# A two-block transformer forward pass on one core: the HGRN scan's steps set half a turn apart, the small gates moved into its first projection, and the low parts of weights issued one panel later

## The chip, the cores and the metric

The kernel runs on one core of one Trainium2 chip. The metric is the device time of one execution in microseconds (us). Before the change three runs took 2718.82, 2721.54 and 2724.38 us, so the median is 2721.54 us.

TensorE (PE) multiplies, VectorE (DVE), ScalarE (ACT) and GpSimd (POOL) work elementwise, and SyncE (SP) issues the weight transfers.

## The reference

Two models run one after the other on 256 tokens of 1024 features, each with two layers, all in float32. The first is attention with three branches; the second has an SSD branch, an HGRN branch and an mLSTM branch, and then a feed-forward part. The change touches the HGRN branch and the small gates of the other two:

```python
q = silu(q_raw);  v = i_in                       # 8 heads of 128
f = lb + (1.0 - lb) * sigmoid(f_raw)             # forward and backward
k = (1.0 - lb) * sigmoid(-f_raw)
o_f = scan(q, k[0], v, log f[0])                 # o_t = sum_s<=t (q_t . prod f . k_s) v_s
o_b = flip(scan(flip(q), flip(k[1]), ...))
o = group_rmsnorm(o_f + o_b) * silu(g_out)
dt = softplus(dt_raw + dt_bias);  A = -exp(a_log)     # small gates: SSD
ig = i + i_bias;  log_f = log_sigmoid(f + f_bias)     # small gates: mLSTM
```

## The kernel before, in words

**Weights.** Every projection is cut into 768 panels of 1024 weights for each partition (512 KB). SP loads panel i into a ring of five slots (`wring`). ACT rounds it to the high part `whi`, DVE subtracts to get the low part `wlo`; both have four slots. PE makes three products for each tile (high by high, high by low, low by high). A panel is two tiles of columns with four chunks of rows, or the like: 24 matmuls.

**Order.** `schedule` writes one list of steps. Each engine's program walks this list and issues, in that order, its own part of every step. Nothing is reordered later: an instruction that waits holds up all that its engine has behind it. `weave((a, 1), (b, 1.2))` interleaves generators: at each turn `a` advances one `yield`, `b` 1.2 on average. A projection (`projB`) yields after each panel and again after its output step.

**Split.** At the step `panel i` the list gets `split` of panel i + 3 (`LEAD`). ACT's half waits until the transfer has landed and until PE is done with panel i - 1, whose slot it takes (`NS` = 4). DVE's half waits for ACT's half. SP's transfer of panel p waits for the low part of panel p - 5.

**HGRN scan.** Four heads at a time (`hg_scan`, twice for each layer), the 256 tokens' decays are built in levels j = 0 to 6. One level has four parts:
- `hg_scale j` (DVE): four multiplies of half of `hgQF`, `hgkf`, `hgQB`, `hgkb` by the products of decays `hgTf` and `hgTb`, and two shorter ones that make the next `hgTf`, `hgTb`.
- `hg_merge j+1`: ACT makes three copies of halves into `hgQm` and `hgKm`, POOL one. It waits for `hg_scale j` and for the products of level j - 1, whose buffers it takes; `hg_scale j+1` waits for it.
- `hg_products j`: eight float32 matmuls of 128x128 (16 instructions) on PE, once `hg_merge j` is done.
- the same step on DVE: two predicated copies from PSUM into `hgA`.

Ahead stand the first product (j = -1) and `hg_split`; behind stand `hg_cross`, `hg_values` and `hg_norm`.

**Order around the scan.** For each layer: the first half's projections (`hg_proj(0)`, 20 panels) alone; then its scan woven with the small gates and the second half's projections (20 panels); then the second scan woven with two gates' projections (16 panels). The small gates are one narrow panel, some 15 short DVE operations, four ACT operations with three different function tables, short matmuls for running sums, and a running maximum in eight steps of four short DVE operations.

`forget_out` stands for two parts: ACT's two sigmoids, and DVE's six operations that scale them.

Of the kernel before, what the change touches and what calls it, by code (L numbers as in the profile page):

```python
# [315 lines left out]
def run(g):  # L316
    for _ in g:
        pass
# [89 lines left out]
def schedule(K, a):  # L408
# [439 lines left out]
    def block2(l, norm):  # L848
# [4 lines left out]
        rms_turn(norm, l, "norm_mix_g_2", uT)  # L853

        def small_gates():
            tb = ar.take("smallT", 256, at=7168)
# [4 lines left out]
            yield  # L861
            do("ssd_skip", c, AB.take())
            yield
            yield
            yield
            do("cumsum_rows", c, AB.take(), AB.take())
# [12 lines left out]
            do("ml_max_cols", c, AB.take())  # L879
            do("store_max", c)  # L880
            yield
# [3 lines left out]
        def hg_proj(hf, B):  # L885
            c0, o = hf * 512, 17920 * hf
            B.q = ar.take("hgq", 1024, at=o)
            yield from projB(w, GQ + c0, 512, uT, features_to(B.q, ACT.Silu))
            fk, kk = B.f, B.kf = ar.take("hgf", 1024, at=o + 1024), ar.take("hgkf", 1024, at=o + 3072)
            yield from projB(w, GF + c0, 512, uT, lambda k, m, u: do("forget_out", c, fk, kk, hf * 4, k, u))  # L890
            fk, kk = B.b, B.kb = ar.take("hgb", 1024, at=o + 2048), ar.take("hgkb", 1024, at=o + 4096)
            yield from projB(w, GF + 1024 + c0, 512, uT, lambda k, m, u: do("forget_out", c, fk, kk, 8 + hf * 4, k, u))
            B.v = ar.take("hgv", 1024, at=o + 5120)
            yield from projA(w, GI + c0, 512, uT, tokens_to(B.v, 512))
            B.g = ar.take("hgg", 1024, at=o + 6144)
            yield from projB(w, GG + c0, 512, uT, features_to(B.g, ACT.Silu))

        def hg_scan(hf, B, W):
# [3 lines left out]
            do("hg_start", B)  # L902
            do("hg_products", B, -1, [AB.take(), AB.take()])
            do("hg_split", B)
            do("hg_merge", B, 0)
            yield
            for j in range(7):
                do("hg_scale", B, j)
                if j < 6:
                    do("hg_merge", B, j + 1)  # L910
                yield
                do("hg_products", B, j, [AB.take(), AB.take()])
                yield
            do("hg_cross", B, [AB.take(), AB.take()])
            ar.give(B.q, B.f, B.b, B.kf, B.kb)
            if hf:
                ar.give(*W.Tf, *W.Tb, *W.QK[1])
            yield
            for h in range(0, 4, 2):
# [145 lines left out]
        B0, B1 = Box(), Box()  # L1065
        run(hg_proj(0, B0))
        yh = ar.take("yh", 2048, at=25104)
        c.sm, c.mxb = ar.take("sm", 688, at=31360), ar.take("mxb", 1024, at=32048)
        c.rows = ar.take("rows", 512, at=33072)

        c.spread = {}
        RS = Slots([c.mxb.part("spread", 0, 512), c.mxb.part("spread", 512, 512), c.rows.again("spread")])

        def spread_rows(i):
            if i < 24:
                c.spread[i] = RS.take()
                do("spread_rows", c, i, c.spread[i])
        s, mxb = c.sm.ap, c.mxb.ap
        c.par = K.parb[:, 128 * l:128 * l + 112]
        c.ds = K.parb[0:1, 128 * l + 112:128 * l + 128].rearrange("p (c j) -> p j c", j=2)  # L1080
        v2 = lambda o, n: s[:, o:o + n].rearrange("p (t k) -> p t k", t=2)
        c.raw, c.z, c.za, c.dts, c.LA, c.ncum, c.R, c.em = (
            v2(0, 128), v2(128, 96), v2(224, 96), v2(320, 96), v2(416, 96), v2(512, 96), v2(608, 32), v2(640, 32))
        c.Dc, c.nA = s[:, 672:680], s[:, 640:672]
        c.ldt = c.z[:, :, 0:32]

        c.mA = mxb[0:8, 0:512].rearrange("p (d t) -> p d t", d=2)
        c.mB = mxb[0:8, 512:1024].rearrange("p (d t) -> p d t", d=2)
        c.nmx = c.mA
        W = hg_work()  # L1090
        weave((hg_scan(0, B0, W), 1), (small_gates(), 0.8), (hg_proj(1, B1), 1.2))

# [425 lines left out]
def scalar_program(e, K, sg, a):  # L1518
# [3 lines left out]

    def split(p):
        w, hi, lo = p.flat
# [205 lines left out]

    def forget_out(c, fk, kk, i0, k, u):
        e.wait_ge(*at(u.full))
# [129 lines left out]
    parts = dict(split=split, load_first=load_first, load_second=load_second, columns=columns, rope_tables=rope_tables,  # L1862
                 lower_bounds=lower_bounds, split_bank=split_bank, split_bank_scaled=split_bank_scaled, features_out=features_out,
# [13 lines left out]
def vector_program(e, K, sg):  # L1877
# [3 lines left out]

    def split(p):
        w, hi, lo = p.flat
# [308 lines left out]
    def small_gates(c):  # L2192
# [11 lines left out]
        e.wait_ge(*now(chain))  # L2204
        e.tensor_tensor(c.za, c.za, c.z, ALU.min).then_inc(*up(chain, ("za", c.l)))
        e.wait_ge(*at(("softplus", c.l)))
        e.tensor_scalar(c.z, c.z, 0.0, None, ALU.max).then_inc(*up(chain))
# [49 lines left out]

    def forget_out(c, fk, kk, i0, k, u):
        e.wait_ge(*at("bounds"))
# [20 lines left out]

    def hg_products(B, j, us):
        for st in range(2):
# [227 lines left out]

    parts = dict(split=split, rope_tables=rope_tables, lower_bounds=lower_bounds, split_bank=split_bank, split_bank_scaled=split_bank_scaled,
                 latent_out=latent_out, latent_norm=latent_norm, kpe_out=kpe_out, mla_rope=mla_rope, scores=scores, weights=weights,
# [3 lines left out]
                 ssd_skip=ssd_skip, cumsum_cols=cumsum_cols, ml_key_gates=ml_key_gates, ml_max_rows=ml_max_rows,  # L2516
                 ml_max_step=ml_max_step, ml_max_negate=ml_max_negate, ml_max_cols=ml_max_cols, forget_out=forget_out, hg_start=hg_start,
                 hg_products=hg_products, hg_split=hg_split, hg_scale=hg_scale, hg_norm=hg_norm, ssd_conv=ssd_conv, ssd_products=ssd_products, ssd_exponents=ssd_exponents, ml_exponents=ml_exponents, ssd_weights=ssd_weights,
                 ssd_outputs=ssd_outputs, ssd_norm=ssd_norm, ml_weights=ml_weights, ml_outputs=ml_outputs, ml_variance=ml_variance, ml_norm=ml_norm,
# [193 lines left out]
```

## Time and profile before

| | |
|---|---|
| median of three runs | 2721.54 us |
| profiled execution, its own time | 2726.25 us |
| its span on the core | 2724.4 us |
| PE busy | 2526.3 us (93%) |
| DVE busy | 1808.3 us (66%) |
| ACT busy | 1433.4 us (53%) |
| POOL busy | 226.7 us (8%) |
| mean granted TensorE clock | 0.967 |
| read from HBM | 422.35 MB |

The span is the time from the first to the last instruction that the profiler saw. PE is busy nearly all the time, so the time goes where PE is idle, or where its clock is granted at half. In the second model layer 0 begins near 1098 us and layer 1 near 1906 us; the HGRN stretch is 1110 to 1372 us in the one and ends at 2182 us in the other.

### The profile page before, as it was taken

To read this page: it belongs to the slowest core of one execution; us is meant where nothing else is said; L and a number is where in the kernel's file an instruction comes from. 1 tells how busy PE (TensorE), PEld (TensorE's weight loads), DVE (VectorE), ACT (ScalarE), POOL (GpSimd) and SP (SyncE) were. 2 spreads that over 40 slices of the span, in tenths; PEclk is the share of its full clock that TensorE was granted. 3 is DMA by queue.
4 is the path that set the end of the run, shared out by engine and by line. 5 is a ranking of instruction groups with operands and counts; after the bars stand their busy time and mean duration, and the time that the engine had idled before them with its cause. 6 is when DMAs were issued, how large, how long until landed. Compare 5 with 4: busy or idle time off the path is not lost.

```text
span 2724.4 us, 42235 instructions
## 1 busy us (share of the span) xinstructions
PE 2526.3 (93%) x17296; PEld 2312.2 (85%) x17296; DVE 1808.3 (66%) x2928; ACT 1433.4 (53%) x2099; POOL 226.7 (8%) x193
## 2 busy tenths in 40 slices
PE   7998999999989999879899979999979899979998
PEld 7887889988779898778899778998878898778997
DVE  4556676555566755657677777875567677776875
ACT  4555545545464544446455534664545556535654
POOL 0000000000000000000024510000000025410000
PEclk9999999999999999889899989999989999989999
DMA  7553456655435566533367635665624467635663
GB/s 226 155 140 102 138 172 191 192 155 162 119 92 166 171 205 202 143 93 109 109 190 185 170 105 172 187 202 172 171 74 114 115 198 196 168 99 173 192 199 131
DMA packets 358958, 426.24 MB, mean 156 GB/s; under 512 B 21208, under 2 KB 286894, under 8 KB 358766
## 3 DMA queue, kind: packets, MB, share of 16 engines
q1 hardware_dynamic: 342890, 401.95, 49.2%
q10 hardware_dynamic: 14068, 15.91, 2.7%
q0 software_dynamic: 1808, 5.69, 0.7%
q8 instruction: 137, 2.24, 0.3%
q14 instruction: 55, 0.45, 0.1%
HBM read 422.35 MB, written 1.15 MB: 155 GB/s over the span
## 4 chain that ended last, share of the span: by engine, by line
PE 68%; DVE 18%; ACT 9%; issue 4%; DMA 1%; ACTq 0%; POOL 0%; DVEq 0%
PE ps L112 66%; DVE wlo L121 4%; ACT whi L118 3%; DVE sE L121 2%; PE ps L115 2%; ACT hgKm L118 1%; DVE hgA L148 1%; ACT E L118 1%; DVE hgQF L121 1%; ACT L118 1%; DVE hgQB L121 1%; DVE E L124 1%; DVE hgkf L121 1%; DVE xN L121 1%; DVE hgkb L121 1%
## 5 line engine op out<-in xcount | busy, mean ns | idle before, releaser
L121 DVE TENSOR_TENSOR wlo<-wring,whi 128x1024 fp32r<-128x1024 f32 x768 | 925.6, 1217 | 581.9 <-ACT whi L118 581.5
L118 ACT ACTIVATE whi<-wring 128x1024 fp32r<-128x1024 f32 x768 | 800.8, 1053 | 419.8 <-PE ps L112 410.7
L112 PE MATMUL ps<-uT,whi 128*128 128x256 f32 x4640 | 835.4, 284 | 12.7 <-DVE uT L121 9.1
L112 PEld LDWEIGHTS ps<-uT,whi 128*128 128x128 f32 x4640 | 723.4, 193 | 20.3 <-issue 19.2
L112 PE MATMUL ps<-uT,wlo 128*128 128x256 f32 x2320 | 654.1, 282 | 0.0
L112 PEld LDWEIGHTS ps<-uT,wlo 128*128 128x128 f32 x2320 | 446.2, 192 | 0.0
L112 PE MATMUL ps<-xT,whi 128*128 128x256 f32 x2112 | 387.6, 287 | 4.7 <-DVE xT L121 4.0
L112 PEld LDWEIGHTS ps<-xT,whi 128*128 128x128 f32 x2112 | 328.6, 191 | 12.2 <-issue 7.8
L112 PE MATMUL ps<-xT,wlo 128*128 128x256 f32 x1056 | 299.4, 284 | 0.0
L112 PE MATMUL ps<-whi,hid 128*128 128x512 f32 x864 | 267.8, 389 | 0.0
L112 PEld LDWEIGHTS ps<-xT,wlo 128*128 128x128 f32 x1056 | 202.9, 192 | 0.5
L112 PEld LDWEIGHTS ps<-whi,hid 128*128 128x128 f32 x864 | 162.2, 188 | 33.3
L112 PE MATMUL ps<-wlo,hid 128*128 128x512 f32 x432 | 168.1, 389 | 0.0
L112 PE MATMUL ps<-whi,xT 128*128 128x512 f32 x384 | 132.2, 406 | 0.0
L124 POOL TENSOR_SCALAR sE<-mxb,sm 128x256 f32<-128x256 f32 x64 | 109.6, 1721 | 270.8 <-DMA mxb<-spread 258.8
L112 PE MATMUL ps<-whi,uT 128*128 128x512 f32 x384 | 127.9, 404 | 0.0
L118 ACT ACTIVATE E<-ps,E 128x256 f32<-128x256 f32 x112 | 52.1, 472 | 119.1 <-DVE E L124 118.9
L112 PE MATMUL ps<-hgQm,hgKm 128*128 128x128 f32 x448 | 67.2, 311 | 40.1 <-ACT hgKm L118 33.0
L118 ACT ACT_TABLE_LOAD x77 | 98.8, 1283 | 3.3 <-issue 1.8
L112 PEld LDWEIGHTS ps<-hgQm,hgKm 128*128 128x128 f32 x448 | 62.6, 222 | 43.2 <-ACT hgKm L118 35.0
L112 PEld LDWEIGHTS ps<-wlo,hid 128*128 128x128 f32 x432 | 81.1, 188 | 16.5
L118 ACT ACTIVATE hgQm<-hgQF 128x512 f32<-128x512 f32 x28 | 17.9, 640 | 138.9 <-DVE hgTb L121 114.9
(377 smaller groups left out, 3670.4 us busy)
## 6 DMA issues: line engine op xcount, KB each, us to landing
wring<-in_w_in SPq DMA_DIRECT2D x346, 512.0 KB, 4.0
wring<-in_mlp_w SPq DMA_DIRECT2D x128, 512.0 KB, 4.4
wring<-in_w_up SPq DMA_DIRECT2D x88, 512.0 KB, 4.4
wring<-in_w_down SPq DMA_DIRECT2D x44, 512.0 KB, 3.9
wring<-in_w_branch SPq DMA_DIRECT2D x32, 512.0 KB, 3.6
wring<-in_w_out SPq DMA_DIRECT2D x32, 512.0 KB, 3.9
wring<-in_mem_w_kv SPq DMA_DIRECT2D x16, 512.0 KB, 5.2
wring<-in_w_br_hg SPq DMA_DIRECT2D x16, 512.0 KB, 4.4
```

What stands on the lines that cost most here:

```text
L112: return self.e.matmul(*p, **k) if self.e else Nothing()
L115: return self.e.transpose(*p, **k) if self.e else Nothing()
L118: return self.e.activation(*p, **k) if self.e else Nothing()
L121: return self.e.tensor_tensor(*p, **k) if self.e else Nothing()
L124: return self.e.tensor_scalar(*p, **k) if self.e else Nothing()
L148: return self.e.copy_predicated(*p, **k) if self.e else Nothing()
```

## The change

Four things change in the list of steps; no arithmetic is added or removed.

1. Steps of the scan. `hg_products` becomes two steps: the matmuls keep the name and come directly behind `hg_scale j` in the list; the copies into `hgA` become `hg_level j`. Between the two there is a yield, and `hg_merge j+1` moves from directly behind `hg_scale j` to behind that yield. So the list reads: scale j, products j, (other work), merge j+1, level j, (other work), scale j+1.
2. `forget_out` is cut in two: DVE's part is `forget_scale`, issued at the next output instead of its own.
3. The small gates are woven into `hg_proj(0)`, seven yields late, and no longer into the first scan. Their DVE part is split in two (`small_gates`, `small_rates`).
4. `split` becomes `split_hi` (panel i + 3, as before) and `split_lo` (panel i + 2). This holds for all 768 panels of both models.

```diff
+        if pend: do("forget_scale", *pend.pop())      # in forget's out()
 ...
             do("hg_start", B)
-            do("hg_products", B, -1, [AB.take(), AB.take()])
             do("hg_split", B)
+            yield
+            us = [AB.take(), AB.take()]
+            do("hg_products", B, -1, us)
             do("hg_merge", B, 0)
             yield
+            do("hg_level", B, -1, us)
             for j in range(7):
+                us = [AB.take(), AB.take()]
                 do("hg_scale", B, j)
+                do("hg_products", B, j, us)
+                yield
                 if j < 6:
                     do("hg_merge", B, j + 1)
-                yield
-                do("hg_products", B, j, [AB.take(), AB.take()])
+                do("hg_level", B, j, us)
                 yield
 ...
-        run(hg_proj(0, B0))
-        weave((hg_scan(0, B0, W), 1), (small_gates(), 0.8), (hg_proj(1, B1), 1.2))
+        weave((hg_proj(0, B0), 1), (small_gates(), 1))
+        weave((hg_scan(0, B0, W), 1), (hg_proj(1, B1), 1.3))
 ...
             for p in panels[i + LEAD:i + LEAD + 1] if i else panels[0:LEAD + 1]:
-                K.steps.append(("split", (p,)))
+                K.steps.append(("split_hi", (p,)))
+            for p in panels[i + LEAD - 1:i + LEAD] if i else panels[0:LEAD]:
+                K.steps.append(("split_lo", (p,)))
```

ACT's order in the first scan of layer 0, before; `sm` are the small gates, `hgQm` and `hgKm` a merge, `hgq` the second half's q:

```order
L118 ACTIVATE hgKm_194<-hgkb_177 128x128x4
L118 ACTIVATE whi<-wring 128x1024
L118 ACT_TABLE_LOAD
L118 ACTIVATE sm_181<-sm_181 128x96
L118 ACT_TABLE_LOAD
L118 ACTIVATE sm_181<-sm_181 128x96
L118 ACT_TABLE_LOAD
L118 ACTIVATE sm_181<-parb 128x32
L118 ACTIVATE whi<-wring 128x1024
L118 ACTIVATE hgQm_191<-hgQF_184 128x64x8
```

The same stretch between two merges after the change:

```order
L118 ACTIVATE hgKm_194<-hgkb_181 128x128x4
L118 ACTIVATE whi<-wring 128x1024 x2
L118 ACT_TABLE_LOAD
L118 ACTIVATE hgf_197<-ps 128x512
L118 ACTIVATE hgkf_198<-ps 128x512
L118 ACTIVATE hgQm_191<-hgQF_184 128x64x8
```

The gates are gone from between the merges; two high parts and the second half's sigmoids stand there. The gates now stand in ACT's order in the first projection:

```order
L118 ACTIVATE whi<-wring 128x1024 x2
L118 ACT_TABLE_LOAD
L118 ACTIVATE sm_176<-sm_176 128x96
L118 ACT_TABLE_LOAD
L118 ACTIVATE sm_176<-sm_176 128x96
L118 ACT_TABLE_LOAD
L118 ACTIVATE sm_176<-parb 128x32
L118 ACT_TABLE_LOAD
L118 ACTIVATE hgf_174<-ps 128x512
```

There they come in front of the sigmoids of the first half's f, for which a fourth table load is added.

DVE's order behind the first product of the first scan, before (`hgKm<-hgkf,hgkb` is `hg_start`, the copy into `hgA` is level -1):

```order
L121 TENSOR_TENSOR wlo<-wring,whi 128x1024
L121 TENSOR_TENSOR hgKm_192<-hgkf_175,hgkb_177 128x1024
L127 COPY hgA_186<-ps 128x4x128 x2
L121 TENSOR_TENSOR hgQF_184<-hgq_173,hgf_174 128x1024
L121 TENSOR_TENSOR hgQB_185<-hgq_173,hgb_176 128x1024
L121 TENSOR_TENSOR wlo<-wring,whi 128x1024
L121 TENSOR_TENSOR hgQF_184<-hgQF_184,hgf_174 128x512
```

And now:

```order
L121 TENSOR_TENSOR wlo<-wring,whi 128x1024 x2
L121 TENSOR_TENSOR sm_176<-ps,sm_176 128x32
L121 TENSOR_TENSOR hgKm_192<-hgkf_175,hgkb_181 128x1024
L121 TENSOR_TENSOR hgQF_184<-hgq_173,hgf_174 128x1024
L121 TENSOR_TENSOR hgQB_185<-hgq_173,hgb_176 128x1024
L121 TENSOR_TENSOR wlo<-wring,whi 128x1024 x2
L127 COPY hgA_186<-ps 128x4x128 x2
L121 TENSOR_TENSOR hgQF_184<-hgQF_184,hgf_174 128x512
```

The copies that wait for PE moved behind the two multiplies that wait for nothing. Which panel a `wlo` belongs to doesn't show in such rows: each is now that of one panel earlier than the one that stood there.

## Rows read from the trace of the kernel before

**Rows 1.** The page's head.

```profile
span 2724.4 us, 42235 instructions
```

**Rows 2.** Waits of PE, whole span: total, times, longest, in us.

```profile
PE ps L112 <- DVE sE L121: 34.4, 20, 5.7
PE ps L112 <- ACT hgKm L118: 33.0, 10, 6.2
PE ps L115 <- DVE E L130: 24.4, 12, 3.9
...
PE ps L112 <- DVE wlo L121: 5.7, 5, 3.8
```

**Rows 3.** Windows: length, busy PE, PEld, DVE, ACT, POOL, clock, DMA, GB/s.

```profile
1110.00:1168.00 58.00, 57.78 (x429) 55.69 (x430) 32.67 (x51) 32.30 (x40) 0.00 (x0) 0.96 0.63 168
1168.00:1372.00 204.00, 173.36 (x1255) 164.79 (x1254) 135.16 (x249) 109.95 (x153) 8.71 (x14) 0.91 0.35 99
1372.00:1460.00 88.00, 88.00 (x746) 87.79 (x745) 63.82 (x92) 47.57 (x60) 14.05 (x6) 1.00 0.68 193
...
1975.00:2182.00 207.00, 175.65 (x1290) 166.30 (x1289) 138.94 (x252) 112.69 (x155) 11.71 (x15) 0.93 0.37 103
```

**Rows 4.** Timeline of PE: start, length, what, idle before.

```profile
1208.70 2.05 PE L112 MATMUL ps<-hgQm,hgKm 128*128 128x128 f32 x8 [6.18 <-ACT hgKm L118]
...
1284.13 2.05 PE L112 MATMUL ps<-hgq,hgKm 128*128 128x128 f32 x16 [1.42 <-DVE hgKm L121]
```

**Rows 5.** Windows behind these two waits.

```profile
1207.00:1217.00 10.00, 5.80 (x25) 5.54 (x26) 5.67 (x9) 5.21 (x7) 0.43 (x1) 0.50 0.29 70
1284.00:1297.00 13.00, 12.03 (x104) 11.83 (x104) 8.56 (x12) 4.02 (x7) 0.76 (x2) 1.00 0.30 94
```

**Rows 6.** Timeline of DVE, one level of the first scan.

```profile
1211.33 1.22 DVE L121 TENSOR_TENSOR wlo<-wring,whi 128x1024 fp32r<-128x1024 f32 x1 [4.65 <-ACT whi L118]
1212.47 1.33 DVE L148 COPY_PREDICATED hgA<-cst,ps 128x512 f32<-128x512 uint32 x2
...
1214.89 0.69 DVE L121 TENSOR_TENSOR hgQF<-hgQF,hgTf 128x512 f32<-128x512 f32 x1
```

**Rows 7.** Timeline of ACT, the same level.

```profile
1217.75 0.63 ACT L118 ACTIVATE hgQm<-hgQF 128x512 f32<-128x512 f32 x1 [5.51 <-DVE hgTb L121]
...
1218.81 0.61 ACT L118 ACTIVATE hgKm<-hgkb 128x512 f32<-128x512 f32 x1
1219.44 1.28 ACT L118 ACT_TABLE_LOAD   x1
...
1221.70 1.06 ACT L118 ACTIVATE whi<-wring 128x1024 fp32r<-128x1024 f32 x1
```

**Rows 8.** Groups of instructions in 1168 to 1372 us.

```profile
L121 DVE TENSOR_TENSOR wlo<-wring,whi 128x1024 fp32r<-128x1024 f32 x38 | 46.2, 1220 | 45.6 <-ACT whi L118 45.6
```

**Rows 9.** Timeline of DVE in the first model's second matrix stage.

```profile
422.42 0.43 DVE L127 CAST hid<-relu 128x512 fp32r<-128x512 f32 x1 [1.63 <-ACT relu L118]
...
428.28 2.36 DVE L121 TENSOR_TENSOR wlo<-wring,whi 128x1024 fp32r<-128x1024 f32 x2
```

**Rows 10.** Timeline of DVE and ACT at a convolution of the SSD branch.

```profile
1426.35 3.60 DVE L130 SCALAR_TENSOR_TENSOR sx<-ps,cols,sx 128x254 f32<-128x254 f32 x8 [0.20 <-ACT sx L118]
...
1425.32 1.00 ACT L118 ACTIVATE sx<-ps,cols 128x256 f32<-128x256 f32 x2
```

**Rows 11.** Timeline of DVE and PE at a softmax of the first model.

```profile
217.49 1.23 DVE L121 TENSOR_TENSOR wlo<-wring,whi 128x1024 fp32r<-128x1024 f32 x1 [2.15 <-ACT whi L118]
...
221.41 0.88 DVE L130 SCALAR_TENSOR_TENSOR E<-E,E 128x256 f32<-128x256 f32 x2
...
222.04 1.21 PE L115 MATMUL ps<-cst,E 128*128 128x128 f32 x4 [3.89 <-DVE E L130]
```

**Rows 12.** Timeline of POOL.

```profile
1372.02 8.36 POOL L124 TENSOR_SCALAR sE<-mxb,sm 128x256 f32<-128x256 f32 x3 [31.55 <-DMA mxb<-spread]
...
1217.79 0.61 POOL L127 COPY hgQm<-hgQB 128x512 f32<-128x512 f32 x1 [10.36 <-DVE hgTb L121]
```

More of the change, by code:

```diff
@@ L853, in block2, with small_pieces, spread_rows @@
         rms_turn(norm, l, "norm_mix_g_2", uT)
+        def small_pieces():
+            c.sm, c.mxb = ar.take("sm", 688, at=31360), ar.take("mxb", 1024, at=32048)
+            c.rows = ar.take("rows", 512, at=33072)
+            c.spread = {}
+            c.ring = Slots([c.mxb.part("spread", 0, 512), c.mxb.part("spread", 512, 512), c.rows.again("spread")])
+            s, mxb = c.sm.ap, c.mxb.ap
+            c.par = K.parb[:, 128 * l:128 * l + 112]
+            c.ds = K.parb[0:1, 128 * l + 112:128 * l + 128].rearrange("p (c j) -> p j c", j=2)
+            v2 = lambda o, n: s[:, o:o + n].rearrange("p (t k) -> p t k", t=2)
+            c.raw, c.z, c.za, c.dts, c.LA, c.ncum, c.R, c.em = (
+                v2(0, 128), v2(128, 96), v2(224, 96), v2(320, 96), v2(416, 96), v2(512, 96), v2(608, 32), v2(640, 32))
+            c.Dc, c.nA = s[:, 672:680], s[:, 640:672]
+            c.ldt = c.z[:, :, 0:32]
+            c.mA = mxb[0:8, 0:512].rearrange("p (d t) -> p d t", d=2)
+            c.mB = mxb[0:8, 512:1024].rearrange("p (d t) -> p d t", d=2)
+            c.nmx = c.mA
+        def spread_rows(i):
+            if i < 24:
+                c.spread[i] = c.ring.take()
+                do("spread_rows", c, i, c.spread[i])
         def small_gates():
+            for _ in range(7):
+                yield
+            small_pieces()
             tb = ar.take("smallT", 256, at=7168)
@@ L861, in small_gates @@
             yield
+            yield
+            do("small_rates", c)
             do("ssd_skip", c, AB.take())
@@ L864, in small_gates @@
             yield
+            do("cumsum_rows", c, AB.take(), AB.take())
             yield
-            do("cumsum_rows", c, AB.take(), AB.take())
             do("cumsum_cols", c, AB.take(), AB.take())
@@ L888, in hg_proj, with forget, out @@
             yield from projB(w, GQ + c0, 512, uT, features_to(B.q, ACT.Silu))
[L889 to L892, printed above, removed]
+            pend = []
+            def forget(fk, kk, i0):
+                def out(k, m, u):
+                    do("forget_out", fk, kk, k, u)
+                    if pend:
+                        do("forget_scale", *pend.pop())
+                    pend.append((c, fk, kk, i0, k))
+                return out
+            B.f, B.kf = ar.take("hgf", 1024, at=o + 1024), ar.take("hgkf", 1024, at=o + 3072)
+            yield from projB(w, GF + c0, 512, uT, forget(B.f, B.kf, hf * 4))
+            B.b, B.kb = ar.take("hgb", 1024, at=o + 2048), ar.take("hgkb", 1024, at=o + 4096)
+            yield from projB(w, GF + 1024 + c0, 512, uT, forget(B.b, B.kb, 8 + hf * 4))
             B.v = ar.take("hgv", 1024, at=o + 5120)
             yield from projA(w, GI + c0, 512, uT, tokens_to(B.v, 512))
+            do("forget_scale", *pend.pop())
             B.g = ar.take("hgg", 1024, at=o + 6144)
@@ L917, in hg_scan @@
                 ar.give(*W.Tf, *W.Tb, *W.QK[1])
+            yield
             yield
@@ L1065, in block2 @@
         B0, B1 = Box(), Box()
-        run(hg_proj(0, B0))
[L1067 to L1090, printed above, removed]
-        weave((hg_scan(0, B0, W), 1), (small_gates(), 0.8), (hg_proj(1, B1), 1.2))
+        weave((hg_proj(0, B0), 1), (small_gates(), 1))
+        W, yh = hg_work(), ar.take("yh", 2048, at=25104)
+        weave((hg_scan(0, B0, W), 1), (hg_proj(1, B1), 1.3))
         def two_gates():
@@ L1521, in scalar_program, with split_hi @@
     cst = K.cst
-    def split(p):
+    def split_hi(p):
         w, hi, lo = p.flat
@@ L2205, in small_gates, with small_rates @@
         e.tensor_tensor(c.za, c.za, c.z, ALU.min).then_inc(*up(chain, ("za", c.l)))
+    def small_rates(c):
+        chain = "dve_gates"
         e.wait_ge(*at(("softplus", c.l)))
@@ L2516, in vector_program @@
                  ssd_skip=ssd_skip, cumsum_cols=cumsum_cols, ml_key_gates=ml_key_gates, ml_max_rows=ml_max_rows,
[L2517 to L2518 removed]
+                 ml_max_step=ml_max_step, ml_max_negate=ml_max_negate, ml_max_cols=ml_max_cols, small_rates=small_rates, forget_scale=forget_scale, hg_start=hg_start,
+                 hg_level=hg_level, hg_split=hg_split, hg_scale=hg_scale, hg_norm=hg_norm, ssd_conv=ssd_conv, ssd_products=ssd_products, ssd_exponents=ssd_exponents, ml_exponents=ml_exponents, ssd_weights=ssd_weights,
                  ssd_outputs=ssd_outputs, ssd_norm=ssd_norm, ml_weights=ml_weights, ml_outputs=ml_outputs, ml_variance=ml_variance, ml_norm=ml_norm,
```

14 lines of the change are left out of this document (8 added, 6 removed).

## The prediction

> **What bounds the kernel now.** I read the table by engine first, then the waits of PE over the whole span, then busy times and clock by stretch, and last the timelines of one level of the scan. The span is 2724.4 us [rows 1] and PE is busy in 93% of it, so a change can win PE's idle time and its slow time, and little else. In the waits of PE the reader is to see that no single wait is large, and that three of the four largest are waits for short DVE and ACT work in scans and softmaxes: 34.4 us for `sE`, 33.0 for the merges `hgKm`, 24.4 for `E`; the low parts `wlo` cost 5.7 [rows 2].
>
> By stretch, the HGRN scans of layer 0 have 204 - 173.4 = 30.6 us of idle PE, and those of layer 1 207 - 175.7 = 31.3; together 62. The clock granted there is 0.91 and 0.93. A mean of 0.91 between the two levels of 1.0 and 0.5 says that 18% of the time was at half; half of that work's time is lost, so about 0.09 x 173 + 0.07 x 176 = 28 us. So 90 us of the two stretches are not PE at its pace, while the stretch before them (57.8 of 58 busy) and the one behind (88.0 of 88, clock 1.00) lose nothing [rows 3]. A wait of 6.2 us ahead of a product is followed by ten microseconds at 0.50, the lower of the two levels (1.2 GHz); one of 1.4 us is followed by thirteen at 1.00 (2.4 GHz) [rows 4, 5]. Long waits are paid twice, short ones once.
>
> Why PE waits is seen in one level. DVE stands idle 4.65 us for a high part, then makes the low part (1.2), two predicated copies (1.3), another low part, and the scaling of the level (from 1214.9 to 1217.7, 2.8 us) [rows 6, 7]. ACT stands idle 5.51 us for that scaling, makes three copies (1217.75 to 1219.4, 1.7 us), a table load of 1.28 with an output, and only then the next high part [rows 7], for which DVE waits again. The two engines take turns: 2.8 + 1.7 + 1.3 (table) + 1.1 (outputs) + 1.1 (high part) + 1.2 (low) + 1.3 (copies) = 10.5 us a level. PE has only 1.7 panels and one product for it. A panel is 24 matmuls at 88.0/746 = 0.118 us, 2.83 us [rows 3], a product 2.05 [rows 4]: 6.9 us. In both scans of layer 0 DVE waited 45.6 us for high parts alone [rows 8].
>
> **The change, part by part.** It is reckoned against the profiled execution's own time, 2726.25 us, which is 4.7 above the median of the runs.
>
> *Steps half a turn apart and low parts later, in the scans.* A low part now stands on DVE where its high part was made a panel ago, so the wait of 4.65 us goes. ACT meets a merge half a turn after the scaling. The loop that is left is scaling, merge, next scaling: 2.8 + 1.7 = 4.5 us, with copies (1.3) and a low part (1.2) beside the merge, so 5.3; PE needs 2.05 + 2.83 = 4.9 with one panel between two products and 7.7 with two. I laid the first scan out in the new order with these durations. From product 1 to product 6 there are 8 panels and 5 products for PE, 33 us; DVE has 5 scalings (13.4), 5 pairs of copies (6.6), 8 low parts (9.2) and 3 scalings of forget gates (1.7 each, 5.1), 34 us. They run side by side and PE waits 1 to 2 us in all. What is late next: at the second scan's start PE has two panels behind the last `hg_norm`, 5.7 us, while ACT's square root with two tables (4), DVE's last multiplies (1.6), a low part and `hg_start` (2.4) take 8; the start costs 1 to 2.5 us and the first level, whose scaling takes 3.7, another 1.5. At the second scan's end `hg_values` and `hg_norm` have no panel between them: 1 us. I leave 8 us of idle for each layer where there were 31: 46 us are won. At the ends: 0, if ACT still holds the merges up, and 62.
>
> *Small gates in the first projection.* Removed from the scan are about 10 us of DVE work, three table loads of 1.28 us with ACT waiting between them, and the narrow panel's turn. Their worst effect is the 6.2 us wait, counted above. In `hg_proj(0)` DVE is busy 32.7 of 58 us and ACT 32.3 [rows 3]: 25 us of room for 10 and for 12 (4 uses of the table load, 5.1, and the waits of the chain). Behind ACT's waiting `sm` operation is queued the high part of a panel that PE wants some 8 us later; the chain of three tables is 4.6 us with `small_rates` 1.5 behind it. PE's matmuls and the narrow panel are moved, not added. Cost 0 to 3 us a layer; I count 1, inside the 8 above.
>
> *Clock.* Waits of up to 1.4 us left it at 1.00 [rows 5], and those that I expect are 0.2 to 2.5. I take 20 of the 28 us; the ends are 0 and 28.
>
> *Low parts a panel later, everywhere else.* This is an unknown with both signs. For it speaks the softmax: DVE waits 2.15 us for a high part, and 4 us later ends the `E` for which PE waits 3.89 [rows 11]. Twelve such waits are 24.4 us; with half of them gone I win 12, and 2 of the `sE` waits. The ends are 0 and 30, with their clock.
> Against it: a low part has now to be ready two panels, 5.66 us, behind the output ahead of it, where it had three. In the matrix stage an output and four additions of 1.2 us stand ahead of it on DVE, from 422.4 to 428.3, and then 1.2 for itself, 7.1 us [rows 9]; with about 1.2 on ACT ahead of them that is 8.3 against 5.66, so that PE must wait 2.6 us, with the clock behind it 4 or 5. That is once in each layer of the first model, and a half of it at each of three other norms and merges. At an SSD convolution ACT takes 1.0, DVE 3.6 [rows 10] and the low part 1.2: 5.9 us against 5.66, 0.3 to 0.8 lost at each of 12. Together 10 + 8 + 5 = 23 us; the ends are 5 and 40. Transfers wait for low parts too: one panel less leaves four, 11 us, for a landing of about 4.
>
> Sum: 46 + 20 + 14 - 23 = 57 us. 2726 - 57 = 2669 for the profiled execution. The runs lie lower by about 3 to 5, so 2666 us.
>
> A rule of the chip can speak against the merge. POOL's copy of a quarter of each merge takes 0.61 us [rows 12], while DVE is idle beside it. Three of POOL's operations that began at 1372.0, with low parts and multiplies on DVE, took 8.36 us, the first of them alone far above the 1.2 of the others [rows 12]. The Trainium skill (GPSIMD Engine Reference, the table of the engine's resources) says that GpSimd's SBUF interfaces are shared with VectorE, with contention when a DVE instruction has two SBUF inputs; the trace agrees, by that 8.36. By this rule POOL's copy would now stand still behind a low part of 1.2 us. In the kernel's own terms: 1.2 + 0.6 is 1.9 against the 1.7 of ACT's three copies, so 0.2 us a level, and 1.4 us where two low parts follow each other. That is 2 to 8 us over four scans, inside my range.
>
> **The rivals.**
> A. Nothing comes of the half turn: outputs still stand ahead of merges on ACT and wait for the end of a panel (0.6 to 1.2 us, then 1.7 of copies), and the next product stands right behind that panel. The order shows such outputs; against it, in my layout a panel stands between in all but a few. At three of seven levels, 2.4 us each in four scans, 29 of the 46 us come back, and 12 of the clock's 20: 2666 + 41 = 2707.
> B. The waits get short but the clock still falls: 2666 + 20 = 2686. For it: it fell after 2.2 us waits too; against it [rows 5].
> C. All goes well: 58 idle, 26 clock, 18 elsewhere and 15 for the low parts: 87 us in place of 57, 2636.
> D. Slower: the lead of two panels is too short wherever an output stands on DVE. Place: the low part behind an output step, some 350 of them. From a delay of 4.4 us behind the panel's end on, PE waits; at 0.4 us each it costs 140 us against the 80 won (46, 20 and 14): 2722 + 60 = 2782; at 0.23 it is even. Against it: most outputs are 1 to 3 us of ACT and DVE work, and `wlo` cost 5.7 us in all with one panel more [rows 2].
> That the change doesn't do what it says can be left out: the order shows it.
>
> **How the numbers follow.** Forecast (2650 to 2680) 0.50; A 0.17; B 0.14; C 0.13; D 0.06. The range runs from C to A, 2636 to 2707; outside lie D and the far halves of A and C, 0.2. About 0.2% (5 us) is what a measurement of this kernel can tell from no change. Slower is D, 0.06; the same is A's far end, 0.04; faster is 0.90.
>
> **What would show it.** In the changed profile the waits for `hgKm` and `hgA` are under 10 us for both layers where they were 43; DVE's wait for high parts in the scans falls from 45.6 to under 20 a layer; the clock of the scans' stretch is at 0.97 or more; `hg_proj(0)` keeps PE over 98% busy; waits for `wlo` rise from 5.7 to some 20 us, most of it at the first model's norms; those for `E` halve. I am wrong if the scans keep a clock under 0.95, or if `wlo` waits pass 50 us.

## The result, and the profile after

The changed kernel takes 2625.98 us (median of four runs, 2622.43 to 2627.59), against 2722.96 for the kernel before. The ratio is 0.9644, with a 95% interval of 0.9627 to 0.966: 97 us faster. Forecast were 2666, in a range of 2636 to 2707: the direction was right, the size too small, and the time lies 10 us below the range. Nearest was rival C (2636). The profiled execution took 2625.02 us, 101 less than that of before.

The head of the page, and PE's waits over the whole span (total in us, times, longest):

```profile
span 2623.2 us, 42231 instructions
```

```profile
PE ps L112 <- DVE wlo L121: 31.9, 21, 4.3
PE ps L112 <- DVE sE L121: 27.5, 15, 6.0
...
PE ps L112 <- ACT hgKm L118: 6.2, 8, 1.6
PE ps L115 <- DVE E L130: 5.7, 4, 2.2
```

Against [rows 2], the merges `hgKm` fell from 33.0 to 6.2 and `E` from 24.4 to 5.7; `sE` lost 7; low parts now cost 31.9 where they cost 5.7. The waits for `hgA`, 10.5 us in all before, are gone.

The same stretches of the program in both traces, cut at the first use of the same panel: first the attention of the first model's two layers, then the HGRN stretch of the second model's two (first projection to the fourth convolution of the SSD branch). Columns as in [rows 3]. Before:

```profile
143.52:353.91 210.39, 196.89 (x1356) 175.67 (x1355) 133.37 (x250) 113.62 (x230) 0.72 (x1) 0.97 0.44 128
570.12:820.49 250.37, 231.80 (x1403) 199.25 (x1402) 152.62 (x289) 137.47 (x269) 3.83 (x5) 0.95 0.43 122
1110.22:1437.70 327.48, 296.84 (x2238) 286.14 (x2239) 214.89 (x363) 177.41 (x235) 22.77 (x20) 0.94 0.47 132
1904.04:2228.29 324.25, 286.84 (x2160) 273.88 (x2158) 214.44 (x362) 178.51 (x239) 24.90 (x22) 0.94 0.47 132
```

After:

```profile
142.53:340.18 197.65, 191.19 (x1355) 170.16 (x1354) 131.46 (x250) 112.36 (x227) 0.72 (x1) 1.00 0.44 134
563.75:799.27 235.52, 225.28 (x1403) 193.48 (x1402) 152.74 (x289) 137.68 (x269) 3.77 (x5) 0.98 0.43 130
1092.87:1383.17 290.30, 280.65 (x2238) 270.41 (x2239) 213.38 (x363) 180.70 (x236) 30.28 (x20) 0.99 0.51 150
1842.26:2132.29 290.03, 274.89 (x2158) 262.95 (x2159) 213.02 (x361) 180.58 (x239) 31.34 (x22) 0.98 0.50 147
```

PE does the same matmuls in both. Its idle time is length less busy; where busy time falls, I put it down to the clock, whose column rises in the same rows. The last line of the table is the span less the four stretches. All in us:

| stretch | length before, after | won | idle | clock |
|---|---|---|---|---|
| two attentions | 460.8, 433.2 | 27.6 | 32.1 to 16.7: 15.4 | 428.7 to 416.5: 12.2 |
| two HGRN stretches | 651.7, 580.3 | 71.4 | 68.1 to 24.8: 43.3 | 583.7 to 555.5: 28.1 |
| all the rest | 1611.9, 1609.7 | 2.2 | | |

The small difference of the rest hides two larger ones. Up to the first HGRN stretch, nearly all of it the first model, the program outside the attentions grew from 649.5 to 659.7 us, by 10.2; behind that, in the second model outside the HGRN stretches, it shrank from 962.4 to 950.0, by 12.4, of which under 3 us are idle time.

In the scans of layer 0 DVE hardly waits for a high part now, 7.3 us where [rows 8] had 45.6 (a window of the trace after from 1153 to 1306 us):

```profile
L121 DVE TENSOR_TENSOR wlo<-wring,whi 128x1024 fp32r<-128x1024 f32 x37 | 45.2, 1232 | 7.3 <-ACT whi L118 7.3
```

One level of that scan on DVE: the low part starts as the scaling ends, with no wait, where it stood idle 4.65 us in [rows 6]; the copies into `hgA` and a forget gate follow.

```profile
1186.72 0.22 DVE L121 TENSOR_TENSOR hgTb<-hgTb 128x64 f32<-128x64 f32 x1
1186.86 1.22 DVE L121 TENSOR_TENSOR wlo<-wring,whi 128x1024 fp32r<-128x1024 f32 x1
1187.99 1.38 DVE L148 COPY_PREDICATED hgA<-cst,ps 128x512 f32<-128x512 uint32 x2
1189.26 0.73 DVE L124 TENSOR_SCALAR hgf<-hgf,lbc 128x256 f32<-128x256 f32 x2
```

New is a wait behind each layer's second scan, where the four splits of `yT` stand ahead of the low part on DVE and of the high part on ACT. First DVE, then PE:

```profile
1312.81 2.69 DVE L121 TENSOR_TENSOR yT<-yh,yT 128x512 fp32r<-128x512 f32 x4 [0.70 <-ACT yT L118]
1315.43 4.82 DVE L121 TENSOR_TENSOR wlo<-wring,whi 128x1024 fp32r<-128x1024 f32 x4
```

```profile
1316.69 0.80 PE L112 MATMUL ps<-uT,whi 128*128 128x256 f32 x2 [4.32 <-DVE wlo L121]
```

### The profile page after: what moved, and what is told of

Read it like the earlier page. It is cut to its first block, busy times and chain, and to the rows that moved or that the text cites. A ratio compares the mean times of both kernels' runs of the same rounds, so it can differ in the third digit from the quotient of the medians.

```text
span 2623.2 us, 42231 instructions
## 1 busy us (share of the span) xinstructions
PE 2481.1 (95%) x17296; PEld 2270.7 (87%) x17296; DVE 1796.4 (68%) x2928; ACT 1442.4 (55%) x2101; POOL 249.5 (10%) x193
## 4 chain that ended last, share of the span: by engine, by line
PE 76%; DVE 13%; ACT 5%; issue 3%; DMA 1%; POOL 1%; SPq 1%; ACTq 0%; DVEq 0%
PE ps L112 75%; DVE wlo L121 3%; PE ps L115 2%; ACT L118 1%; POOL sE L124 1%; DVE sE L121 1%; ACT whi L118 1%; DVE xN L121 1%; ACT hgKm L118 1%; SPq L154 1%; DVE sz L130 0%; DVE sx L124 0%; ACT rms L118 0%; ACT E L118 0%; DMA memN<-in_mem 0%
## 5 line engine op out<-in xcount | busy, mean ns | idle before, releaser
L112 PEld LDWEIGHTS ps<-uT,whi 128*128 128x128 f32 x4640 | 712.1, 190 | 33.3 <-issue 19.9
L112 PEld LDWEIGHTS ps<-whi,uT 128*128 128x128 f32 x384 | 72.1, 188 | 17.3 <-DVE wlo L121 1.4
L112 PEld LDWEIGHTS ps<-whi,xT 128*128 128x128 f32 x384 | 72.2, 188 | 16.3 <-issue 1.5
L112 PE MATMUL ps<-whi,merged 128*128 128x512 f32 x256 | 81.2, 394 | 3.4 <-DVE wlo L121 3.4
```

Source lines behind the costliest of these rows:

```text
L112: return self.e.matmul(*p, **k) if self.e else Nothing()
```

## The experiments

The change has four parts: half turn (H), gates into the first projection (G), cut of `forget_out` (C), late low parts (L). All kernels with H or G below hold C too, but for the last one; the interval stands behind each ratio. Each ratio is to the kernel before, run beside it on the same chip; between chips I compare ratios and not times.

**Late low parts taken back** (H, G, C stay).

```
-            for p in panels[i + LEAD - 1:i + LEAD] if i else panels[0:LEAD]:
+            for p in panels[i + LEAD:i + LEAD + 1] if i else panels[0:LEAD + 1]:
                 K.steps.append(("split_lo", (p,)))
```

> The changed kernel, with the low part of a weight issued directly behind its high part again (panel i + 3); the half turn and the gates' place stay. Theory H (the half turn carries the scans; late low parts are a separate trade, won in the softmaxes, lost at norms and splits): the scans give back 10 to 25 us, since DVE waits again for high parts, the softmaxes give back some 24 us, the 26 us of waits for low parts go with their clock (some 35): 2626 + 18 + 24 - 35 = 2633, range 2620 to 2650. Rival L (DVE's wait for high parts was what held the scans, and the late low part carries their gain): idle PE of the two HGRN stretches goes back above 45 us, 2675 or more.

Measured: 2686.1 us, ratio 0.9864 (0.9848 to 0.9881): 60 us of the 97 are lost. The HGRN stretches are 302.1 and 305.9 us long, idle 18.7 and 24.3:

```profile
1108.72:1410.82 302.10, 283.45 (x2238) 272.22 (x2239) 214.67 (x363) 180.32 (x236) 31.08 (x20) 0.98 0.51 143
1882.73:2188.59 305.86, 281.59 (x2160) 268.40 (x2159) 214.09 (x362) 181.59 (x240) 32.58 (x22) 0.95 0.50 139
```

Theory H missed by over 50 us. By time rival L (2675 or more) holds; by its mark for the idle time (above 45; it is 43) it just doesn't: 43.8 us of the 71 won in these stretches survive without late low parts, 28 go, and the rest of the loss is outside them.

**Late low parts alone**, put on the kernel before (the same two lines, the other way).

> The kernel before, with the low part alone issued a panel later, for all 768 panels; steps of the scan and small gates as before. Theory H: the softmaxes win 24 us, norms and splits lose 30 to 35, the scans win 10 to 25 of their 90: 2723 - 24 + 33 - 18 = 2714, range 2700 to 2730. Rival L: the scans win most of their 87 us by this alone: 2660 or less. Rival D of the prediction (the lead of two is too short wherever an output stands): over 2730.

Measured: 2639.3 us, 0.9697 (0.9681 to 0.9713): theory H falls, rival L (2660 or less) holds. One part of four brings some 82 of the 97 us. The HGRN stretches, with steps and gates as before, are 295.1 and 296.5 us long:

```profile
1090.23:1385.33 295.10, 279.79 (x2239) 269.90 (x2239) 213.88 (x363) 177.97 (x235) 32.74 (x20) 0.98 0.51 147
1847.15:2143.60 296.45, 277.50 (x2158) 265.77 (x2159) 213.82 (x361) 177.61 (x238) 33.83 (x22) 0.97 0.51 144
```

**Gates back in the first scan** (H, C, L stay).

```
-            for _ in range(7):      # in small_gates()
-                yield
 ...
-        weave((hg_proj(0, B0), 1), (small_gates(), 1))
+        run(hg_proj(0, B0))
 ...
-        weave((hg_scan(0, B0, W), 1), (hg_proj(1, B1), 1.3))
+        weave((hg_scan(0, B0, W), 1), (small_gates(), 0.8), (hg_proj(1, B1), 1.3))
```

> The changed kernel, with the small gates woven into the first scan again (weight 0.8), the half turn and the late low parts kept. Theory H: in the scan the three table loads and the ten DVE operations stand between scaling and merge again, at two or three levels; 5 to 12 us a layer with the clock behind the longest wait: 2640 to 2650. Rival G (with half a turn of room the gates fit into the scan as well, so their move brought nothing): 2626 to 2631.

Measured: 2644.44 us, 0.9714 (0.9697 to 0.9731), as theory H had it. It isn't better than late low parts alone (0.9697), though it holds the half turn and the cut besides. Against the same kernel without the half turn (the run with the cut alone, below, 0.9657) it is some 15 us slower, and the intervals don't overlap; the two differ in the weight of the second half's projections too, 1.3 against 1.2.

**The scan's steps back in the old order** (G, C, L stay): `hg_merge` again directly behind `hg_scale`, products and copies together, the added yields gone.

> The changed kernel, with the scan's steps in the order of before (scaling and merge side by side, product and its copies side by side half a turn later), the gates' move and the late low parts kept. Theory H: each level is held up by scaling, then merge, then PE again: 30 to 60 us come back, half of it clock, 2656 to 2686. Rival L: the scans stay within 15 us of the changed kernel, 2641 or less.

Measured: 2613.26 us, 0.9603 (0.9584 to 0.9621), some 12 us below the changed kernel, and the intervals don't overlap. Theory H falls for good: the half turn costs time where low parts are late. Its HGRN stretches:

```profile
1094.54:1379.02 284.48, 277.69 (x2238) 267.09 (x2239) 214.45 (x363) 177.62 (x235) 32.49 (x20) 0.99 0.54 153
1838.96:2125.55 286.59, 274.13 (x2158) 262.01 (x2159) 214.44 (x361) 177.23 (x238) 33.62 (x22) 0.99 0.53 150
```

They are 9.3 us shorter together than after the change. Behind the second scan, where the change brought a wait of 4.32 us, two short ones are left (the outputs come a yield earlier):

```profile
1312.53 0.51 PE L112 MATMUL ps<-uT,whi 128*128 128x256 f32 x2 [0.79 <-DVE wlo L121]
...
1316.07 0.50 PE L112 MATMUL ps<-uT,whi 128*128 128x256 f32 x2 [0.54 <-DVE wlo L121]
```

**Gates and cut only**, put on the kernel before.

> The kernel before, with the small gates (and the cut of the forget gates' step that goes with them) in the first projection, and nothing else: scan steps and low parts as before. The kernel with half turn and gates stood at 2686, the one before at 2724. Theory T (without late low parts the half turn does most of what those two do): 2705 to 2718. Rival G (it was the gates' move): 2680 to 2695.

Measured: 2715.76 us, 0.9986 (0.9977 to 0.9995): 4 to 5 us, inside theory T's 2705 to 2718. The longest wait for a merge fell from 6.2 to 3.9 us, but there are 16 of them for 10, and together they cost 39.6 where they cost 33.0. Its trace shows the old ring of waits without the gates in it. ACT:

```profile
1211.54 0.63 ACT L118 ACTIVATE hgQm<-hgQF 128x512 f32<-128x512 f32 x1 [5.10 <-DVE hgTb L121]
...
1212.59 0.61 ACT L118 ACTIVATE hgKm<-hgkb 128x512 f32<-128x512 f32 x1
1213.11 1.99 ACT L118 ACTIVATE whi<-wring 128x1024 fp32r<-128x1024 f32 x2
```

and DVE:

```profile
1214.19 1.22 DVE L121 TENSOR_TENSOR wlo<-wring,whi 128x1024 fp32r<-128x1024 f32 x1 [2.75 <-ACT whi L118]
1215.33 1.34 DVE L148 COPY_PREDICATED hgA<-cst,ps 128x512 f32<-128x512 uint32 x2
1216.57 1.20 DVE L121 TENSOR_TENSOR wlo<-wring,whi 128x1024 fp32r<-128x1024 f32 x1
1217.70 0.68 DVE L121 TENSOR_TENSOR hgQF<-hgQF,hgTf 128x512 f32<-128x512 f32 x1
```

The merge stands ahead of the high parts on ACT; DVE waits for the first of these, and only behind it come the copies and the next scaling, for which ACT then waits. A low part that doesn't need this high part takes most of DVE's wait out of the ring, in the old order of the scan's steps as in the new one; the table behind the next run has the sizes.

**The half turn only** (with the cut).

> The changed kernel with the low parts back at panel i + 3 and the small gates back in the first scan: of the change only the half turn is left (with the cut of the forget gates' step). By now stand: low parts alone 2639, gates alone 2716, half turn and gates 2686, before 2721. Theory T (each of half turn and late low part alone ends the taking of turns, so that they don't add): the half turn alone wins 25 to 35 us, 2686 to 2696. Rival N (it won only together with the gates' move): 2705 or more.

Measured: 2687.73 us, 0.9876 (0.986 to 0.9892), as theory T had it. With gates moved (2686.1 against 2715.8) or without, the half turn is worth 30 us or a little more if low parts are early, and it costs 11 to 15 if they are late (0.9644 against 0.9603, 0.9714 against 0.9657).

The waits inside the two HGRN stretches of each trace tell what each edit takes away (us, both layers added; the scalings are `hgTb` and, at a scan's start, `hgQB`):

| kernel | DVE for high parts | ACT for scalings | PE for merges (`hgKm`, ACT) |
|---|---|---|---|
| before | 155.6 | 133.5 | 33.0 |
| G, C | 163.3 | 143.5 | 39.6 |
| H, G, C (late low parts taken back) | 132.6 | 71.8 | 15.6 |
| H, C (half turn only) | 146.6 | 60.6 | 20.2 |
| L (late low parts alone) | 49.5 | 93.7 | 0.8 |
| G, C, L (steps back) | 51.5 | 80.5 | 0.8 |
| H, G, C, L (the change) | 48.4 | 39.9 | 6.2 |

Two of the rows that it is added up from, for layer 0, are these: late low parts taken back, then steps back.

```profile
DVE wlo L121 <- ACT whi L118: 65.9, 40, 5.1
PE ps L112 <- ACT hgKm L118: 7.7, 3, 3.9
```

```profile
DVE wlo L121 <- ACT whi L118: 25.8, 21, 2.9
PE ps L112 <- ACT hgKm L118: 0.4, 1, 0.4
```

The two edits act on different links of one ring. The half turn takes away 6% (without the gates' move) or 19% (with it) of DVE's wait for high parts and half of ACT's wait for the scalings; PE's wait for merges falls to 61% or 39%. The late low part takes away two thirds of DVE's wait, and PE's wait for merges is gone. Both work on the same wait of PE, and once the late low part has ended it, the half turn has next to nothing left to bring.

**The half turn in the first scan alone** (all else as changed).

> The changed kernel, with the half turn kept in the first scan of each layer and taken back in the second, its additional yield ahead of the last outputs too. Theory S (the half turn is worth something only beside the twenty panels of the first scan, and costs at the second scan's start and end): by stretch the first scans keep 5.9 and 3.9 us against the run with all steps back, the second scans keep that run's 6.4 and 2.8 us and its 6.7 and 4.1 us behind the scan: 2613 - 10 = 2603, range 2598 to 2608. Rival M (the first scan's gain is only time moved to another stretch): 2610 to 2618.

Measured: 2621.43 us, with runs from 2612.28 to 2627.44; 0.9637 (0.962 to 0.9653). That can't be told from the changed kernel (0.9644), and isn't under the one with all steps back (0.9603). The six microseconds that I had read by stretch from single executions weren't there: 2603 was missed.

**Where late low parts pay: only in the HGRN stretches, and only outside.** Both are the kernel before, with the low part's lead chosen by panel number.

```
+LATE = set(range(320, 378)) | set(range(543, 602))      # the second run has EARLY = this set
+EARLY = set(range(768)) - LATE
 ...
+            to = i + LEAD + (i + LEAD in EARLY)
+            while K.low < min(to, len(panels)):
+                K.steps.append(("split_lo", (panels[K.low],)))
+                K.low += 1
```

> The kernel before, with the low part a panel later for the weights of the two HGRN stretches alone (some 117 of 768 panels). By stretch, the run with all low parts late won 32 us between the first projection and the convolutions of layer 0 and 26 in layer 1. Theory S (places are independent of each other): 2721 - 55 = 2666, range 2658 to 2674. Rival W (the late low part wins in the scans only because DVE comes there with work done ahead): 2690 or more.

> The kernel before, with the low part a panel later everywhere but in the two HGRN stretches: the other half of the run with low parts alone. Theory S: softmaxes 27 us won, norms and merges of the first model 9 lost, the other scans of the second model 12 won: 2721 - 29 = 2692, range 2684 to 2700; with the run for the scans alone it adds up to the 82 of all low parts. Rival F (as forecast, outside the scans late low parts cost more than they bring): 2721 to 2735.

Measured: 2664.27 us, 0.9791 (0.9776 to 0.9806), in the stretches alone, and 2692.67 us, 0.9903 (0.9886 to 0.9919), outside alone. By the medians 57 and 28 us; the sum of 85 is that of all low parts late (2639.3 against 2724.3). Theory S held for both: the gains of different places add up, and 57 of the 85 us lie in the HGRN stretches. The waits of PE for `sE`, 34.4 us in all before, are 26.5 with late low parts outside alone and 36.2 with those in the stretches alone: they too go with the late low part.

**Two panels late**, on the kernel with the steps back.

> The run with all scan steps back (2613), with the low part two panels later than its high part (panel i + 1). It tests the prediction's rival D one step further. Theory D (an output step of 4 us or more of ACT and DVE work then stands ahead of a low part that PE wants in 2.8 us): the waits for low parts pass 100 us, 2680 or more. Rival (the outputs are short and DVE has 30% of idle time): waits under 60 us, and the softmaxes win once more: 2605 to 2630.

Measured: 2931.09 us, 1.0771 (1.0752 to 1.0791): 318 us slower than the one it was made from. Waits of PE:

```profile
PE ps L112 <- DVE wlo L121: 267.6, 173, 5.7
PE ps L112 <- DVE sE L121: 19.7, 6, 6.1
```

This is the prediction's rival D, one panel further on: the low part behind outputs, 173 times, 1.5 us each. The waits for `sE` fell once more, from 27.8 to 19.7; that is little beside it.

**Mixed leads**: back at panel i + 3 for the panels of ten places where PE had waited for a low part or the time by stretch had risen (the expectation says 67; the list in the kernel holds 59), first with the half turn in the first scan, then with all steps back.

> The run before this one, with the low part back at panel i + 3 for some 67 panels at ten places where TensorE waited for it or the time by stretch rose (both norms and merges of the first model, behind the second scan, four others), a panel later for all others. Theory P (place decides: a low part a panel later pays where DVE waits for high parts, costs where an output step stands ahead of it): the waits for low parts fall from 31 to under 18 us and 10 to 15 us are won with the clock behind them: 2590, range 2585 to 2595. Rival Q (the early low parts make DVE wait for ACT there, and the next output is late instead): 2600 or more.

> The run with all scan steps back (2613), with the low parts back at panel i + 3 at the ten places of the mixed run. Theory P: 8 to 15 us are won again and the half turn isn't needed: 2598 to 2606, level with the mixed run (2604) or under it. Rival (the half turn of the first scan was worth its 6 us a layer): 2608 to 2614.

Measured: 2604.21 us, 0.9572 (0.9553 to 0.9591), and 2597.36 us, 0.9544 (0.953 to 0.9559). Theory P holds: the first lies 17 us below the run that it was made from (its 2590 started from 2603, which was wrong), the second 16. The second is the fastest of all, 29 us below the changed kernel. Its waits of PE:

```profile
PE ps L112 <- DVE sE L121: 25.8, 13, 6.1
PE ps L115 <- DVE rN L124: 18.3, 4, 9.2
PE ps L112 <- DVE wlo L121: 17.3, 20, 3.8
```

Low parts are at 17.3 where they were 31.5 in the run that it was made from, and what the late ones had won in `sE` stays.

**Gates and cut apart, beside late low parts.** Low parts alone gave 0.9697, with gates and cut 0.9603. The first run has the cut alone, the second the gates' move alone.

> Late low parts and the cut of the forget gates' step (its DVE part at the next output); scan steps and small gates as before. Late low parts alone stood at 0.9697 of the time before, with cut and gates' move at 0.9603: 26 us apart. Theory C (the cut does it: with late low parts alone DVE waits 3.7 us for sigmoids ahead of the copies into hgA, and PE 6.0 for these): 2613 to 2620. Rival G (the gates' move does it): 2632 to 2640.

> Late low parts and the small gates in the first projection, with the forget gates' step whole again (its DVE part at its own output); scan steps as before. Theory C (the cut does it): 2632 to 2640, with waits for hgA back at 8 us or more. Rival G (the gates' move does it): 2613 to 2620.

Measured: cut alone 2627.97 us, 0.9657 (0.9633 to 0.9681); gates alone 2646.09 us, 0.9715 (0.9699 to 0.9732). Neither rival is right, and theory C's own mark, waits for `hgA` of 8 us or more without the cut, fails too: these waits are 13.9 us with late low parts alone, and gone in both runs. The cut wins some 11 us (0.9657 against 0.9697; the intervals only just touch). The gates' move wins nothing by itself (0.9715 against 0.9697), and some 15 with the cut (0.9603 against 0.9657, with the weight of 1.3 for 1.2 in it). The trace of the gates without the cut names the place. In the first projection DVE waits for the sigmoids of `forget_out`, which stand on ACT behind three table loads of the gates and a fourth of their own. A copy out of PSUM that the small gates' matmuls need (`sm`, line 127) stands on DVE behind this wait, and PE waits for it. First DVE, then PE:

```profile
1123.70 0.74 DVE L124 TENSOR_SCALAR hgf<-hgf,lbc 128x256 f32<-128x256 f32 x2 [5.40 <-ACT hgf L118]
```

```profile
1127.86 3.59 PE L112 MATMUL ps<-cst,sm 128*32 128x256 f32 x8 [4.91 <-DVE sm L127]
```

With gates and cut (the run with the steps back) the only wait of PE in that projection, behind its start, is 0.47 us. So the cut and the place of the gates have to be judged together.

## Why the prediction was right or wrong

**What bounds the kernel: right.** Idle time and half clock in scans and softmaxes were what there was to win, and the HGRN stretches gave 71 us. What was named as the sign of it came: `hgKm` and `hgA` at 6.2 us (under 10), DVE's waits for high parts at 7.3 and 7.0 in the windows of the scans (under 20), the clock of the scans at 1.00 and 0.98 (0.97 or more). The second window takes in a wait of 4.3 us behind the scan, the first doesn't:

```profile
1153.69:1306.16 152.47, 147.60 (x1175) 141.70 (x1173) 120.13 (x189) 97.22 (x132) 18.66 (x14) 1.00 0.44 128
1918.40:2085.62 167.22, 158.03 (x1246) 151.68 (x1245) 129.15 (x200) 106.73 (x143) 27.07 (x18) 0.98 0.45 131
```

**The scans' terms: sizes right, the cause wrong.** Forecast were 46 us of idle and 20 of clock; the table above has 43 and 28. But the step priced the half turn and the late low parts as one thing, and told it as the half turn's work, with rival A (2707) hanging on the half turn. The runs show that the late low parts would have done it: alone they shorten these stretches by 60 us (327.5 and 324.3 to 295.1 and 296.5), and with gates and cut by 81. The ring of 10.5 us that I summed up had DVE's wait for a high part as one of its links, and I hadn't asked what each edit by itself does to the ring. The half turn leaves most of that link as it was (at least 81% of the wait) and some half of PE's waits for merges; the late low part alone ends these (0.8 us of 33.0 are left). Beside it the half turn only adds its price: 6.2 us of waits for merges for 0.8, and the wait of 4.3 us behind each second scan. The 8 us of idle a layer that I had set for the second scan's start and end hold a part of this price.

**The small gates: right in the projection, wrong as to why.** `hg_proj(0)` keeps PE busy for 59.88 of 61 us (98.2%), as forecast:

```profile
1091.00:1152.00 61.00, 59.88 (x458) 55.80 (x457) 43.10 (x105) 42.61 (x57) 0.00 (x0) 0.99 0.56 161
```

That rests on the cut of `forget_out`, which the prediction gave no price of its own. Without it the move costs what it wins. In the scan the prediction took the gates' table loads for the cause of the longest wait, 6.2 us; with them gone and nothing else changed the waits for merges cost more than before.

**Rival C, near by luck.** Its 2636 is the nearest of the numbers, but its terms aren't what came: 84 us in the scans for 71, 18 elsewhere for 28, and 15 lost to low parts where 2 were won.

**Softmaxes: too small.** 14 us were forecast, 27.6 came. The idle time was nearly right (15.4), the clock of 12.2 was left out of the value and stood only in the far end. The row was there to read: 0.97 and 0.95 in the two stretches before, so about 0.03 x 197 + 0.05 x 232 = 18 us of half clock. All of it is the late low parts' work: with these alone the two stretches are 433.3 us long, as after the whole change. I had argued that long waits are paid twice, and did it for the scans alone.

**Low parts elsewhere: the step that failed.** It stood at 23 us of loss; the rest of the program came out 2.2 us shorter, and 2.7 shorter with late low parts alone, so it is these and not the other three parts. The step held two parts of the program that came out differently. Up to the first HGRN stretch the loss is there, 10.2 us, where 18 were forecast for the first model. In the second model, outside the HGRN stretches, 5 us of loss were forecast and 12.4 were won. With late low parts alone it is 7.5 lost and 10.2 won; these are single executions, so a difference of 2 or 3 us between them says nothing. The norm's price was right in kind: the matrix stage waits 3.03 us at 417.7 us, forecast 2.6, and the clock is at 0.67 in the ten microseconds from 417 on.

```profile
417.74 0.80 PE L112 MATMUL ps<-xT,whi 128*128 128x256 f32 x2 [3.03 <-DVE wlo L121]
```

At the convolutions I had set 0.3 to 0.8 us at each of twelve, and PE waits there only twice, 0.22 and 0.44 us. And nothing was set against the losses, though the `sE` waits in the other scans go with the late low part as those of the softmaxes do: 2 us were counted (with the softmaxes), 7 came. The rest of the 12.4 us is busy time, some 10 us, which I put down to the clock; no run takes it apart further. Waits for `wlo` rose to 31.9, not 20, and only half of the rise of 26 lies in the first model: two waits of 4.3 lie behind the second scans, where the splits of `yT` had not been looked at. So my terms of this step were each a loss, and its sign was wrong. Of the 44 us that 57 fell short of 101, this step makes 25, the softmaxes 14, the HGRN stretches 5.

**The clock: right in kind.** In layer 0's window above, at 1.00, PE waits 1.48 us at 1239.7 and 1.47 at 1251.1. Behind the 4.32 us at 1316.7 the clock falls: the four microseconds from 1317 on are at 0.50, the lower of the two levels (1.2 GHz), and the ten around it have a mean of 0.66:

```profile
1314.00:1324.00 10.00, 7.31 (x45) 7.31 (x46) 6.29 (x8) 5.15 (x7) 10.00 (x6) 0.66 0.61 186
```

Rival B (2686) had no ground: the clock in the HGRN stretches is 0.98 to 0.99.

**POOL beside DVE: the trace bears the rule out, the price didn't come.** POOL's share of the merge takes 1480 ns in the middle where it took 614 before (all of the HGRN scans, min/median/max):

```profile
L127 POOL COPY hgQm<-hgQB x28: 616/1480/2670, 1160.6 to 2042.9; 128x512 f32<-128x512 f32 x28
```

In the trace of before the same row reads 613/614/672. But it isn't the half turn that does it: with the steps back the median is 1482. The copy takes 1.48 us where a low part, with its two inputs, runs beside it (at 1187.08, the low part from 1186.86 shown above). Beside two low parts in a row it takes 2.66:

```profile
1241.81 2.35 DVE L121 TENSOR_TENSOR wlo<-wring,whi 128x1024 fp32r<-128x1024 f32 x2
1242.03 2.66 POOL L127 COPY hgQm<-hgQB 128x512 f32<-128x512 f32 x1 [38.95 <-DVE hgQB L121]
```

In the run with the steps back one took 0.67 at 1206.71, where DVE had one-input multiplies of a forget gate. So the trace agrees with the rule of the Trainium skill (GPSIMD Engine Reference, Specifications) that the two engines contend when DVE reads two SBUF inputs. The 2 to 8 us for it were not seen: 1.48 us is shorter than ACT's 1.7 for the other three copies, and nothing in the trace waits for POOL's copy. The evidence in the prediction was weaker than it said: [rows 12] gives three operations together, 8.36 us, and not the first alone. The trace has 5.65 us for the first, then 1.5 and 1.2.

**Rival D: refuted here, and near.** At a lead of two panels low parts cost 32 us of waits, at one panel 268 (steps back in both).

## What to carry to other kernels

When engines take turns in a ring, write down each link and ask for every edit by itself how much of the wait at the bottleneck it takes away. Edits on different links of one ring don't add: here one of them ended PE's wait for merges, and the other then only brought its costs. Issuing work for an engine right behind that on which it depends makes it wait in order, and a buffer's slack is better spent on a distance between the two, up to the point where the outputs ahead of it are longer than what is left; the lead is best set place by place. A wait long enough to lower the clock is to be priced twice everywhere, not only in the stretch one is looking at.

## What the runs showed of the hardware

POOL's copy made no headway, by its times, while a DVE operation with two SBUF inputs ran. A 128x512 copy of 0.61 us took 1.48 when it began 0.91 us before DVE was through with a low part (1187.08, DVE's next at 1187.99), and 2.66 when it began 2.05 before (1242.03, next at 1244.08): what was left of DVE's work and then 0.6, within 0.05. Four of POOL's multiplies (128x256) took 9.22 us from 1313.3 us on, beside splits and low parts of DVE, 2.3 each in the mean, where two at 1322.5 took 2.42:

```profile
1313.32 9.22 POOL L124 TENSOR_SCALAR sE<-mxb,sm 128x256 f32<-128x256 f32 x4 [34.50 <-DMA mxb<-spread]
```

Runs of one kernel spread by up to 15 us (2612 to 2627 for the half turn in the first scan alone), and the mean clock of these two was 0.986 and 0.983. Differences of 6 us a stretch between single executions, as I took them for that kernel, are within this.
